# Attention of two layers: wide products taken out, probabilities turned by plain products

## The reference, cut to what matters

```
def swa_sink_attention(q, k, v, sinks):      # kind "a": window of 128 keys, blocks of 128 queries
    s = jnp.einsum('bnqhgd,bnkhd->bnhgqk', qb, kk) * (D ** -0.5)      # 8 heads, D = 64, 256 keys
    s = jnp.where(mask, s, NEG)
    m = jnp.maximum(s.max(-1, keepdims=True), sink)
    pr = jnp.exp(s - m)
    denom = pr.sum(-1, keepdims=True) + jnp.exp(sink - m)
    o = jnp.einsum('bnhgqk,bnkhd->bnqhgd', pr / denom, vv)

def dsa_sparse_attention(q, k, v, qi, ki, wi, k_top):                 # kind "b": the 128 best keys of a query
    idx_score = sum over 8 heads of relu(qi . ki) * wi, causal
    _, sel = lax.top_k(idx_score, k_top)
    s = q . k[sel] * (D ** -0.5);  pr = softmax(s);  o = pr @ v[sel]
```

## Time and profile before

| | |
|---|---|
| median of 3 runs | 2417.19 us (2416.0 to 2421.27) |
| the profiled execution's own time | 2411.12 us |
| its span | 2409.4 us |
| PE busy | 2159.8 us, 8629 instructions |
| DVE busy | 966.4 us |
| ACT busy | 594.9 us |
| wide products of the layers (L2096) | x256 |
| attention of layer 0 in the span | 985.8 to 1128.5 us |

### The profile page before, as it was taken

How to read it: one execution, slowest core, us unless ns; L and a number is a source line. 1 busy time by engine, 2 the same in 40 slices (tenths; PEclk the granted TensorE clock), 3 DMA queues, 4 the chain that set the end, 5 groups by cost and what they waited for, 6 DMA issues and landing times. The chain is left out here.

```text
span 2409.4 us, 24842 instructions
## 1 busy us (share of the span) xinstructions
PE 2159.8 (90%) x8629; PEld 1409.3 (58%) x8629; DVE 966.4 (40%) x1735; ACT 594.9 (25%) x1122; POOL 113.2 (5%) x175
## 2 busy tenths in 40 slices
PE   3986788299999869999999999999999999999995
PEld 1543544244444345655478887875555557888784
DVE  1564952221111158662522222344855252222335
ACT  1121221011111112343223332222234232333221
POOL 2000000201011110000100000001000000000001
PEclk8996998599999988999999999999899999999998
DMA  8207012358887460002103333232000211333320
GB/s 282 104 10 272 1 53 106 110 221 314 316 308 307 163 260 1 1 19 96 36 18 104 88 103 122 96 121 94 0 6 14 97 53 35 99 92 103 115 97 35
DMA packets 154637, 269.43 MB, mean 112 GB/s; under 512 B 12224, under 2 KB 109680, under 8 KB 141360
## 3 DMA queue, kind: packets, MB, share of 16 engines
q1 hardware_dynamic: 147696, 258.46, 30.4%
q0 software_dynamic: 6848, 9.77, 1.3%
HBM read 257.64 MB, written 23.14 MB: 117 GB/s over the span
## 5 line engine op out<-in xcount | busy, mean ns | idle before, releaser
L231 PE MATMUL bank<-ht_hi,gate_up_hi 128*128 128x512 f32 x704 | 274.1, 389 | 2.9 <-ACT arena L1218 2.9
L232 PE MATMUL bank<-ht_lo,gate_up_hi 128*128 128x512 f32 x704 | 273.9, 389 | 0.0
L233 PE MATMUL bank<-ht_hi,gate_up_lo 128*128 128x512 f32 x704 | 273.9, 389 | 0.0
L1985 PE MATMUL bank<-arena 128*128 128x512 f32 x512 | 225.2, 593 | 3.7 <-DVE arena L1527 3.7
L2045 PE MATMUL bank<-arena 128*128 128x512 f32 (+3 forms) x640 | 200.0, 475 | 7.4 <-ACT arena L1111 7.4
L2045 PEld LDWEIGHTS bank<-arena 128*128 128x128 f32 x640 | 118.9, 204 | 85.1 <-issue 75.2
L1985 PEld LDWEIGHTS bank<-arena 128*128 128x128 f32 x512 | 95.0, 191 | 111.1 <-issue 107.1
L231 PEld LDWEIGHTS bank<-ht_hi,gate_up_hi 128*128 128x128 f32 x704 | 132.1, 188 | 31.4 <-issue 3.8
L232 PEld LDWEIGHTS bank<-ht_lo,gate_up_hi 128*128 128x128 f32 x704 | 132.1, 188 | 27.4
L233 PEld LDWEIGHTS bank<-ht_hi,gate_up_lo 128*128 128x128 f32 x704 | 132.1, 188 | 27.2
L231 PE MATMUL bank<-down_hi,product_hi 128*128 128x512 f32 x352 | 138.2, 393 | 3.5 <-DVE arena L1732 3.5
(11 more groups left out here) (319 smaller groups left out, 3135.3 us busy)
## 6 DMA issues: line engine op xcount, KB each, us to landing
gate_up_whole<-w_gu SPq DMA_DIRECT2D x88, 512.0 KB, 5.0
arena<-w_gate_e SPq DMA_DIRECT2D x32, 1024.0 KB, 4.9
arena<-w_up_e SPq DMA_DIRECT2D x32, 1024.0 KB, 7.6
arena<-w_down_e SPq DMA_DIRECT2D x32, 1024.0 KB, 9.7
arena<-w_ada SPq DMA_DIRECT2D x12, 2048.0 KB, 11.7
down_whole<-w_down SPq DMA_DIRECT2D x44, 512.0 KB, 3.5
arena<-w_in SPq DMA_DIRECT2D x4, 2048.0 KB, 15.1
arena<-w_o SPq DMA_DIRECT2D x2, 4096.0 KB, 14.1
```

What stands on the lines that cost most here:

```text
L231: pe.matmul(ps, xh, wh, start=start, stop=False)
L232: pe.matmul(ps, xh, wl, start=False, stop=False)
L233: return pe.matmul(ps, xl, wh, start=False, stop=stop)
L1985: ins = pe.matmul(bank[s % 2][:], XW[s % 2][:, c], ring[s][:, :, c], start=c == 0, stop=c == C8 - 1)
```

## The change

In scores() of the layers the loop of two wide products is gone. In turn_p() of the layers the call of turn2 (transposes) is replaced by plain products with the f32 identity: the piece of the probabilities is the stationary operand, the identity the moving one. The bank, the waits and the signal stay as they were. All other turns stay transposes, the first block keeps its own wide products, and FILLERS stays 2 for it.

```
-                    for _ in range(FILLERS):
-                        pe.matmul(ps[:], ident_b, own_mask.unsqueeze(1).broadcast_to([P, 4, P]), start=True, stop=True)
                     pe.matmul(ps[:, 0:w], turned["q" + kind, h // 2][p0:p0 + HD, t * P:(t + 1) * P], keys[p0:p0 + HD, k0:k0 + w],
                               start=True, stop=False)
...
                 def turn_p(n):
                     key = UNITS[n]
                     u2.evacuated(pe, ("s",) + key, l)
-                    turn2(("pT",) + key, [Pr2[:, n % 4, k * P:(k + 1) * P] for k in range(width(n) // P)])
+                    ps = u2.begin(pe, ("pT",) + key, l)
+                    for k in range(width(n) // P):
+                        ins = pe.matmul(ps[:, k * P:(k + 1) * P], Pr2[:, n % 4, k * P:(k + 1) * P], ident, start=True, stop=True)
+                    u2.full(ins, ("pT",) + key)
```

## The result

The changed kernel takes 2478.33 us (median of 4 runs, 2459.58 to 2482.63) against 2416.79 for the kernel before (4 runs, 2416.0 to 2421.27): a ratio of 1.0243, 95% interval 1.0215 to 1.027. It is 2.4% slower where 24 us, 1%, less was forecast. The profiled execution took 2475.82 us with a span of 2474.1.

The account below looks back on a forecast made before the run. PE was taken to set the pace, DVE close behind. Per layer 30.7 - 16.3 = 14.4 us, less 1.4 (narrow chain) and 1.0 (DVE), gives 12.0, 24 for both: median 2393 us, range 2386 to 2401 (0.60), wider 2379 to 2413 (about 0.8).

Parts of the forecast that it names:

- item (c): PE's 2.67 us wait for take_o behind unit 19: unchanged end, small gain behind it set against slower return to full clock.
- The paragraph on the clock: PE in the 256-key beat: values and scores stay, gaps do not grow, so PE stays the pacing engine despite half-clock risk.
- rival (1): Clock falls in units 3 to 31 for want of wide products: 256-key units take 2.5 us, total 2442; chance 0.12.
- The gap of the wide products: Time from first wide product to score in each layer unit: 0.42 to 0.53 us saved, taken as 0.48.
- The plain tile: Turning probabilities on PE: 0.23 us a tile against 0.11 transposed, extra 0.12, on 136 tiles a layer.
- factor of four: Skill's claim on f32 transposes: a plain tile would take 0.44 us, extra 0.33; the prediction took twice instead.
- The sum: PE's gain per layer: 64 x 0.48 - 136 x 0.12 = 14.4 us, before corrections.
- the forecast case: Gap 0.45 to 0.51, extra 0.11 to 0.13, corrections 3 to 2 us per layer: 2386 to 2401 us, chance 0.60.
- Rival (4): Gain cancels, by extra near 0.17 a tile or half-clock pieces behind waits: within 5 us of before; chance 0.05.
- The chain of narrow units: Narrow units hang on a PE, DVE, ACT chain: 2.26 us for two instead of 2.74, giving back 1.4 us per layer.
- rival 3: DVE takes over: units 3 to 31 gain nothing, 12 us gained in all, 2405 us; chance 0.14.
- The units of 512 keys: Widest units: four plain tiles eat what the wide products free, so no gain; beat stays at 3.09 us.

Follow-up runs that it names:

- wide_plain: Kernel before with its wide products kept and probabilities turned by plain products instead of transposes: 2441.53 us, ratio 1.0107.
- bridge2_plain: Changed kernel plus eighteen wide products a layer in PE's waits (three in step 7, five in step 13, ten behind unit 19): 2387.34 us, ratio 0.9869.
- bridge_plain: Changed kernel plus ten wide products a layer, where PE would wait for take_o behind unit 19: 2406.13 us, ratio 0.9955.
- wide_20_22_plain: Changed kernel with the two wide products back in units 20, 21 and 22 of each layer only: 2415.32 us, ratio 0.9988.
- eighteen_elsewhere: Changed kernel plus eighteen wide products a layer in steps 9, 16 and 17, where PE does not wait: 2450.23 us, ratio 1.0181.
- late_kb_plain: Changed kernel plus wide products in steps 7 and 13 only, with kb turned a step later and some qb turns moved: 2392.93 us, ratio 0.9896.
- bridge2_turned: Kernel before with only eighteen wide products a layer, in PE's waits (steps 7, 13, behind unit 19), transposes kept: 2450.13 us, ratio 1.0156.
- no_bridge_19_plain: Changed kernel plus wide products in steps 7 and 13 but none behind unit 19: 2474.57 us, ratio 1.024.

## Why the prediction was wrong

**The step that failed** is the end of item (c): a small gain behind the wait for take_o was put "against a slower return to full clock", so that the slower return was priced at nothing. The paragraph on the clock saw that afterwards the same work without the wide products "has to bring it back", but argued only from what holds the clock, PE's gaps that do not grow, and rival (1) got 0.12. The gaps didn't grow, and the clock did hold at 1.00 up to unit 19, as argued. What it costs when nothing brings the clock back is what was left out: half clock for some 100 us in each layer, and 91 us in all, 2478.33 against the 2387.34 of the same kernel with its waits filled.

The rows spoke for the risk. In both half-clock stretches of the earlier trace rows PE is busy for 8.00 of 8.00 us (the "short waits for ACT" of the index scores are not in that stretch), so gaplessness alone is no argument. And only layer 0 was looked at for the return. In layer 1 of the same trace, with the wide products in place, it took 7 us:

```profile
1791.00:1792.00 1.00, 0.25 (x1) 0.25 (x2) 0.69 (x1) 0.00 (x0) 0.00 (x0) 0.68 0.00 0
1792.00:1798.00 6.00, 6.00 (x22) 3.56 (x21) 1.99 (x5) 2.00 (x5) 0.00 (x0) 0.50 0.01 3
1798.00:1799.00 1.00, 1.00 (x7) 0.66 (x7) 0.00 (x0) 0.00 (x0) 0.00 (x0) 0.90 0.00 0
```

Rival (1) is what happened, but not as priced. It was placed on units 3 to 31, and it began at 20 and lasted to about 45; it was priced 1.5 times the beat, 2.5 us, and the beat of 256 keys at half clock is 3.08: scores, tiles and values all take nearly twice as long. For 512 keys it is 5.0 us against 3.1. Its 2442 us were 36 too few.

**The gap of the wide products.** Values to score are 0.48 us now (1008.99 to 1009.47), against 1009.32 - 1008.40 = 0.92 with them (the values start at 1008.40 there). That is 0.44 saved a unit, where I took 0.48: inside the bounds, near the lower one.

**The plain tile.** Two take 0.50 us against 0.23, four 0.95 (1137.24 to 1138.19 in the changed kernel) against 0.44: an extra of 0.13 each, where I took 0.12. The row of the same shape was the right one. The Trainium skill's factor of four ("TensorE: Matmul & The Clock Gate", section Terms) is out: the factor here is 2.2. But wide_plain cost 24 us by the medians, 29 by the profiled executions, and not 272 x 0.13 = 35. Two things are seen in its trace: in kind "b" a tile costs less, 0.11 (the beat of 512 keys is 3.53 us, 1103.82 to 1107.35, against 3.09), and PE's wait of 0.77 us for ACT's copy in step 13 of the kernel before is gone, so tiles ahead of it lie in time that was idle.

**The sum** of the two would be 64 x 0.44 - 136 x 0.13 = 10.5 us a layer. With the clock held, first to last score in layer 0 takes 127.3 us (989.1 to 1116.4, bridge2_plain) against 137.7 (986.4 to 1124.0): 10.4 less (11.8 in layer 1), where 12.0 was forecast. The run's 2387.34 lies by the low end of the 2386 to 2401 given for the forecast case. So what was forecast is the time of the changed kernel with its waits filled. Rival (4) had a slip: an extra of 0.17 a tile would still have gained some 10 us; it cancels near 0.21.

**The chain of narrow units** was right: two of them take 2.33 us (1156.0 to 1158.3) where 2.26 was worked out. **DVE** (rival 3) didn't become the bound: its cover was thin but held, and what shows of it is the wait of step 13, 0.97 us where it was 0.77 before. It lies behind take_o, and matters for the clock and hardly for its own length. **The units of 512 keys** gain nothing at full clock, as forecast: 3.1 us in bridge2_plain.

**The range** reached to 2413, since 0.16 for slower was left outside it. With a fall of the clock already in the rows, and nothing in the trace to show the remaining work bringing it back, the chance should have been near one half.

## What to carry to other kernels

When work on PE is taken out that seems idle, look at each place where PE waits, and ask of each what brings the clock back behind it, not only whether the steady beat is dense enough to hold it. In this kernel, with plain tiles, eighteen such products a layer, placed where PE waits, did what 128 did before, at next to no cost; breaking up the longest wait by the order of the work did nearly as well as the ten that had filled it. Judge the two halves of a change apart: here the plain tiles were a loss of 24 us with the wide products in place, and taking the wide products out lost 37 us more or, with the waits filled, gained 54.

## What the runs showed of the hardware that was not expected

- The clock fell at PE's wait behind unit 19 wherever it was up and the wait not filled: waits of 2.24 to 2.67 us, both layers of seven profiles. It fell in the wait, at its end or up to about 1 us behind it.
- At waits of about 1 us it went either way. With plain tiles it fell at the 0.96 us of step 13 in both layers of two profiles (bridge_plain, wide_20_22_plain), and held across 0.97 in both layers of two others (the changed kernel, eighteen_elsewhere) and across 0.86 and 0.52 in late_kb_plain. With transposes it fell behind waits of 0.83, 0.71 and 0.49 us, and held across 0.70 in layer 1 of bridge2_turned.
- It fell with hardly a wait, too: in late_kb_plain at 1110, among the narrow units, with PE busy for 4.98 of the 5 us before.
- At half clock PE can be busy without a gap for 90 us, with f32 products on 64 and 128 rows, and stay there (no_bridge_19_plain, 1036 to 1126). Inside the attention and without wide products, the clock rose in units of 512 keys with four plain tiles each (the changed kernel and no_bridge_19_plain, both layers; eighteen_elsewhere, layer 1), and once already at unit 24 (eighteen_elsewhere, layer 0).
- Other work brought it back at once. Ahead of layer 1's attention in the changed kernel PE waits 4.89 us and the clock falls as well; it is back after 3 us, by 1779, with nothing on PE but these transposes and plain products of 128 columns:

```profile
1775.28 1.97 PE L2033 MATMUL bank<-arena 128*128 128x128 f32 x8 [4.89 <-DVE arena L1598]
1777.04 2.67 PE L2045 MATMUL bank<-arena 128*128 128x128 f32 x16
```

- The products of the attention, begun at full clock, can keep it there: from 1024.5 to 1120 in bridge2_plain it reads 1.00. So for the same work the clock depends on where it was.
- Plain products in place of transposes made the difference between 2450 and 2387 us (bridge2_turned, bridge2_plain), though each tile takes 0.11 to 0.13 us longer.
- Why these mixes of work fall on either side was not settled; no run here takes columns, rows, transposes and short waits apart.
